# Delta rule: a 32-wide block inverse grown from the right, with the product W kept beside it

## The chip, the cores and the metric

One NeuronCore of one Trainium2 chip runs the whole program. The metric is the device time of one execution in microseconds, the median of the runs shown. Everything is float32; the large products are made from two rounded parts each (below).

## The reference, cut to what matters

One decoder layer: 256 tokens of width 2048 go through a wide input projection, two token mixers (gated DeltaNet and differential attention), their merge, an output projection with layer norm, and a SwiGLU feed-forward network with a second layer norm. The change is in the DeltaNet mixer, and there in one triangular solve:

```python
# per head and per chunk of C = 64 tokens; decay, beta, g as given
a_mat = jnp.where(strict, jnp.einsum('bhncd,bhnsd->bhncs', k_beta, k) * decay, 0.0)
rhs = jnp.concatenate([v * beta, k_beta * jnp.exp(g)[..., None]], axis=-1)
sol = lax.linalg.triangular_solve(a_mat + jnp.eye(C), rhs, left_side=True, lower=True, unit_diagonal=True)
u, w = sol[..., :dv], sol[..., dv:]
```

There are 16 heads and 4 chunks. The kernel does not solve; it forms the inverse T of (I + A) for each 64 x 64 block and multiplies by it.

## The kernel before, in words

**The stream of large products.** All weights pass through the core as 512 KB tiles of 256 x 512 numbers, in one fixed order, in a ring of four. For each tile ScalarE rounds the weights (`whi`, the function `split`, L800), VectorE takes the rest (`wlo`, L1204), and TensorE makes 12 matmuls of 512 columns (`gemm_tile`): high x high, high x low and low x high, for 2 blocks of rows by 2 blocks of tokens. `AHEAD = 3` tiles are split ahead of the one in use.

**Bodies and slots.** 32 tiles make a body, four groups of 8. A group accumulates into a pair of PSUM banks and is then copied out. After each tile of a body comes a *slot* 0 to 31: TensorE makes the tile's 12 matmuls, and then the small work that is written down for that slot. VectorE in each slot first makes its split, then (in this order) the scan step, the build step, the convolution and the turns of the slot; ScalarE likewise. Each engine works its list strictly in that order, and the engines are tied by counting semaphores only. The first four bodies (one for each four heads) carry the DeltaNet work. The first body is written out, the next three are one loop: scan of batch j-1 in slots 0 to 6, convolutions at slots 8 to 26 (`CONV_SLOTS`), build of batch j in slots 12 to 28. Four bodies with the differential attention follow, one for the last gate, then the branch, output and feed-forward projections.

**The inverse of before.** A batch has 8 matrices of 128 x 128 (4 heads by 2 token halves), each with two 64 x 64 blocks, each of those with two 32 x 32 blocks on its diagonal. `sub(q)` is the q-th 32-wide band. In slot 15 VectorE forms `AT` (the transposed A), takes the pairs on its diagonal blocks and forms the first `TTc` (transposed inverse) and `Tc` (its transpose). Rounds 0 to 3 double the inverted width from 2 to 32. A round has two TensorE places, one slot apart, slots 17 to 24: the even slot multiplies `AT` by `Tc` into a bank, VectorE masks that into `Pc`; the odd slot multiplies `Pc` by `TTc`, VectorE subtracts it from `TTc` and transposes into `Tc`. Each of these places has 32 products of 32 x 32 x 32, four independent ones (q = 0 to 3) side by side for each of the 8 matrices. The fifth round (slots 25 and 26) joins two 32-wide inverses to a 64-wide off-diagonal block, with 16 products a place. A float32 product is two MATMUL records in the trace.

**What is behind it.** In slot 25 ScalarE copies the diagonal blocks to `TTf` and `T` (`act_tt`). In slots 27 and 28 two places of 64 x 64 products join the 64-wide halves; the second one (`B<-TTf,Pm` and `B<-Pm`) waits for ScalarE's copies into `Pm` (`act_p21`), which stand on ScalarE's list behind the SiLU (L903) of the convolution of slots 24 and 26. VectorE also turns V blocks (L1421, `V_TURN`) and, in the loop, blocks of the output of the batch before (L1492, `OT_TURN`), at fixed slots.

`ch(...)` is a VectorE instruction followed by VectorE's own wait for its end.

Of the kernel before, what the change touches and what calls it, by code (L numbers as in the profile page):

```python
# [18 lines left out]
ALU = mybir.AluOpType  # L19
# [21 lines left out]
PV_SLOTS = [5, 11, 17, 23]  # L41
OH_SLOTS = [9, 15, 21, 27]
OT2_SLOTS = [11, 17, 23, 29]
CONV_LINKS, BUILD_LINKS, SCAN_LINKS, DA_LINKS = 12, 13, 7, 25
OT_SLOTS = (12, 14)
OT_TURN = {11: 3, 12: 4, 14: 2, 18: 1, 20: 3, 21: 3}
OT_HI = 29
V_TURN = {21: 1, 22: 3, 23: 3, 27: 3, 28: 2, 29: 2, 30: 1, 31: 1}
TURN = range(1, 7)
# [4 lines left out]
ROWS = range(2, 6)  # L54
WARM = 2
LATE_LO = 4
ROUNDS = 5
TPG = KC // TK
RING = 4
AHEAD = 3  # L60
# [39 lines left out]
def build(nc, xT, xrow, weights, w_ab, consts, early, params, lam_in, ln_in, out):  # L100
# [8 lines left out]
    with ctx:  # L109
# [14 lines left out]
        T = tmp("T", [P, 8, CH])  # L124
        Pm = tmp("Pm", [P, 8, CH])
        Tc = tmp("Tc", [P, 8, SB])
        TTc = tmp("TTc", [P, 8, SB])
        Pc = tmp("Pc", [P, 8, SB])
        masks = tmp("masks", [P, 7, SB])
        vr = tmp("vr", [P, 2, HB, P])  # L130
# [56 lines left out]
        B4 = [b[:, :].rearrange("p (h d) -> p h d", h=HB) for b in B]  # L187
        B8 = [b[:, :].rearrange("p (h d) -> p h d", h=8) for b in B]
        C8 = [b[:, 0:8 * SB].rearrange("p (h d) -> p h d", h=8) for b in B]

        def conv_bank(kind, half):

# [52 lines left out]
        def end_at(s):  # L245
# [23 lines left out]
            dve_lnT dve_x1 pe_x1T act_x1f act_x1T dve_x1T pe_y act_beta act_glo act_var dve_var act_root act_sig act_xn pro_chain ln_chain""".split()  # L269

        counted = """pe_conv dve_conv act_silu dve_cw act_tap
            dve_g rows pe_dt act_decay pe_ktok act_sqk dve_ktail pe_kk dve_at dve_t act_tt pe_p dve_p pe_t
            pe_p21 act_p21 pe_x21 act_x21 dve_vT dve_v pe_kq dve_qk
            pe_z dve_vn pe_so act_s act_o0 pe_ks dve_r pe_o1 dve_o1 pe_qtok act_osq act_sqq
            dve_oh dve_od pe_oT act_oT dve_oT
# [121 lines left out]
        def _(pe):  # L397
# [112 lines left out]
            def dn_build(j, s):  # L510
# [18 lines left out]
                if s == 14:  # L529
# [4 lines left out]
                            kc = cT[:, 0, h, t * P:(t + 1) * P]  # L534
                            last = mm(B4[2 + t][:, h, :], kc, kc)
                    last.then_inc(N["pe_kk"], 1)
                if 17 <= s < 17 + 2 * ROUNDS:
                    r, odd = divmod(s - 17, 2)
                    if not odd:
                        pe.wait_ge(N["dve_t"], 1 + (ROUNDS + 1) * j + r + 1)  # L540
                        waits_end()
                        for i in range(8):
                            if r < ROUNDS - 1:
                                for q in range(4):
                                    a = sub(q)
                                    last = mm(C8[1][a, i, :], AT[a, i, a], Tc[a, i, :])
                            else:
                                for q in (0, 2):
                                    last = mm(C8[1][sub(q + 1), i, :], AT[sub(q), i, sub(q + 1)], Tc[sub(q), i, :])
                        last.then_inc(N["pe_p"], 1)  # L550
                    else:
                        pe.wait_ge(N["dve_p"], 1 + ROUNDS * j + r + 1)
                        waits_end()
                        for i in range(8):
                            if r < ROUNDS - 1:
                                for q in range(4):
                                    a = sub(q)
                                    last = mm(C8[2][a, i, :], Pc[a, i, :], TTc[a, i, :])
                            else:
                                for q in (0, 2):  # L560
                                    b = sub(q + 1)
                                    last = mm(C8[2][sub(q), i, :], Pc[b, i, :], TTc[b, i, :])
                        last.then_inc(N["pe_t"], 1)
                if s == 27:
                    pe.wait_ge(N["dve_t"], 1 + (ROUNDS + 1) * (j + 1))
                    pe.wait_ge(N["act_tt"], 1 + j + 1)
                    waits_end()
                    for i in range(HB):
                        mm(B8[1][CH:P, i, :], AT[0:CH, i, CH:P], T[0:CH, i, :])
                        last = mm(B8[1][0:CH, HB + i, :], AT[0:CH, HB + i, CH:P], T[0:CH, HB + i, :])  # L570
                    last.then_inc(N["pe_p21"], 1)
# [226 lines left out]
        def _(act):  # L798
# [106 lines left out]
            def dn_build(j, s):  # L905
# [23 lines left out]
                                                        accum_out=d_("ss")[:, i:i + 1])  # L929
                        last.then_inc(N["act_sqk"], 1)  # L930
                if s == 25:
                    act.wait_ge(N["dve_t"], 1 + (ROUNDS + 1) * j + ROUNDS)
                    for q in range(4):
                        a = slice(q * SB, (q + 1) * SB)
                        copy(TTf[a, :, a], TTc[a])
                    for q in range(2):
                        a = slice(q * SB, (q + 1) * SB)
                        last = copy(T[a, :, a], Tc[a])
                    last.then_inc(N["act_tt"], 1)
                if s == 27:  # L940
                    act.wait_ge(N["dve_t"], 1 + (ROUNDS + 1) * (j + 1))
                    act.wait_ge(N["act_tt"], 1 + j + 1)
                    copy(Pm[0:CH, 0:HB, :], TTf[CH:P, HB:8, CH:P])
                    act.wait_ge(N["pe_p21"], 1 + j + 1)
                    copy(Pm[CH:P, 0:HB, :], B8[1][CH:P, 0:HB, :])
                    copy(Pm[0:CH, HB:8, :], B8[1][0:CH, HB:8, :]).then_inc(N["act_p21"], 1)
# [253 lines left out]
        def _(dve):  # L1200
# [56 lines left out]
            def prologue(s):  # L1257
# [7 lines left out]
                    tt(pz[0:4 * HEADS, 3, :], ident[0:4 * HEADS, 0:2 * HEADS], ident[0:4 * HEADS, 2 * HEADS:4 * HEADS],  # L1265
                       ALU.add).then_inc(N["dve_two"], 1)
                if s == 11:
                    m0, e0 = CONST["pairs"][0], CONST["eye"][0]
                    for q in range(4):
                        a, f = slice(q * SB, (q + 1) * SB), q % 2 * SB  # L1270
                        V.tensor_copy(masks[a, 0:6, :], cst[a, m0:m0 + 6 * CH].rearrange("p (m c) -> p m c", c=CH)
                                      [:, :, f:f + SB])
                        V.tensor_copy(masks[a, 6, :], cst[a, e0 + f:e0 + f + SB])
                if s == 4:
                    a0 = CONST["negdist"][0]
                    pro(ts(c("same"), cst[:, a0:a0 + P], -1e9, ALU.is_ge))
                    pro(tt(c("after"), c("same"), ident, ALU.subtract))
                    pro(ts(c("same"), c("after"), -1.0, ALU.mult, 1.0, ALU.add))
                    V.tensor_copy(after_r[:, :], c("after"))
                    lv = vda[:, 0, 0:4 * CH].rearrange("p (a b d) -> p a b d", a=2, b=2)  # L1280
                    pro(tt(vda[:, 1, 0:2 * CH].rearrange("p (a d) -> p a d", a=2), lv[:, :, 0, :], lv[:, :, 1, :], ALU.mult))
                    V.tensor_reduce(lam[:, :], vda[:, 1, 0:2 * CH].rearrange("p (a d) -> p a d", a=2), X, ALU.add
                                    ).then_inc(N["dve_lam"], 1)
# [81 lines left out]
            def dn_build(j, s, ch):  # L1365
# [11 lines left out]
                    seed(d_("rk"), d_("ss")).then_inc(N["dve_ss"], 1)  # L1377
                if s == 14:
                    dve.wait_ge(N["act_decay"], 1 + j + 1)
                    dve.wait_ge(N["pe_p21"], 1 + j)  # L1380
                    ch(tt(AT[:, :, :], decm[:, :, :], bc(d_("e"), P), ALU.mult))
                if s == 15:
                    dve.wait_ge(N["pe_kk"], 1 + j + 1)
                    for t in range(TOK):
                        last = tt(AT[:, 4 * t:4 * t + 4, :], B4[2 + t], AT[:, 4 * t:4 * t + 4, :], ALU.mult)
                    last.then_inc(N["dve_at"], 1)
                    dve.wait_ge(N["dve_at"], 1 + j + 1)
                    for q in range(4):
                        a = slice(q * SB, (q + 1) * SB)
                        last = tt(TTc[a], AT[a, :, a], rep(masks[:, 0, :], 8)[a], ALU.mult)  # L1390
                    ch(last)
                    ch(tt(TTc[:, :, :], rep(masks[:, 6, :], 8), TTc[:, :, :], ALU.subtract))
                    V.transpose(flat(Tc[:, :, :]), flat(TTc[:, :, :])).then_inc(N["dve_t"], 1)
                if 17 <= s < 17 + 2 * ROUNDS:
                    r, odd = divmod(s - 17, 2)
                    if not odd:
                        dve.wait_ge(N["pe_p"], 1 + ROUNDS * j + r + 1)
                        if r < ROUNDS - 1:
                            tt(Pc[:, :, :], C8[1], rep(masks[:, r + 2, :], 8), ALU.mult).then_inc(N["dve_p"], 1)
                        else:  # L1400
                            V.tensor_copy(Pc[:, :, :], C8[1]).then_inc(N["dve_p"], 1)
                    else:
                        dve.wait_ge(N["pe_t"], 1 + ROUNDS * j + r + 1)
                        if r < ROUNDS - 1:
                            ch(tt(TTc[:, :, :], TTc[:, :, :], C8[2], ALU.subtract))
                            V.transpose(flat(Tc[:, :, :]), flat(TTc[:, :, :])).then_inc(N["dve_t"], 1)
                        else:
                            for q in (0, 2):
                                a, b = (slice((q + o) * SB, (q + o + 1) * SB) for o in range(2))
                                ins = ts(TTf[a, :, b], C8[2][a], -1.0, ALU.mult)  # L1410
                            ch(ins)
                            V.transpose(T[SB:CH, :, 0:SB], TTf[0:SB, :, SB:CH]).then_inc(N["dve_t"], 1)
                if s == 25:
                    ch(tt(decm[:, :, :], decm[:, :, :], rep(c("same"), 8), ALU.mult))
                if s in V_TURN:
# [525 lines left out]
```

## Time and profile before

| | |
|---|---|
| median of 3 runs | 1940.16 us (1940.04 to 1940.58) |
| span of the profiled execution | 1937.5 us; the profile lists no device time of its own, so the distance from the runs' median is 2.7 us |
| granted TensorE clock, mean | 0.998 of full speed |
| TensorE busy | 1922.7 us, 99% |
| VectorE busy | 1365.1 us, 70% |
| ScalarE busy | 935.0 us, 48% |
| the four DeltaNet bodies | about the first 460 us |

In an answer of the trace "x64" is the number of records that were merged in the row, and the time in brackets is how long the engine was idle before it, with what ended that. The chain is the work that ended last, followed back from the end, each piece with its start, its length and its engine and line. All small products are recorded at the helper's line L399, so they are told apart by their tiles.

### The profile page before, as it was taken

How to read it: one execution, taken by the hardware profiler on the slowest of the kernel's cores; microseconds unless marked ns; L12 is line 12 of the kernel's file. 1: busy time of each engine (PE TensorE's matmuls, PEld its weight loads, DVE VectorE, ACT ScalarE, POOL GpSimd, SP SyncE). 2: the span in 40 equal slices, each digit the busy share in tenths (PEclk: the TensorE clock that was granted, in tenths of full speed). 3: DMA queues.
4: the chain of work that ended last, by engine and by line, in shares of the span. 5: the costliest groups of instructions: out<-in, count | busy, mean ns of one | idle time of the engine just before them, and what ended most of it. 6: DMA issues, size and time to landing. Idle time of an engine off the chain costs nothing.

```text
span 1937.5 us, 33061 instructions
## 1 busy us (share of the span) xinstructions
PE 1922.7 (99%) x11140; PEld 1581.1 (82%) x11140; DVE 1365.1 (70%) x1961; ACT 935.0 (48%) x1331; POOL 101.1 (5%) x296
## 2 busy tenths in 40 slices
PE   9999999999999999999999999999999999999997
PEld 7888887888888888888888888888888888888886
DVE  7779889797857777776566766577675466665556
ACT  6555565554455545455544445644443444443442
POOL 0102020010101111111000000000000000000000
PEclk9999999999999999999999999999999999999999
DMA  7444444444554545455655676555555555656555
GB/s 267 154 142 158 149 152 142 154 153 142 186 179 159 188 161 191 159 189 174 190 192 194 216 239 200 181 194 191 191 194 195 194 193 188 196 195 194 194 189 174
DMA packets 98013, 353.19 MB, mean 182 GB/s; under 512 B 10832, under 2 KB 11120, under 8 KB 97776
## 3 DMA queue, kind: packets, MB, share of 16 engines
q1 hardware_dynamic: 97904, 351.65, 55.4%
q8 instruction: 79, 1.29, 0.3%
q14 instruction: 30, 0.25, 0.0%
HBM read 349.51 MB, written 2.10 MB: 181 GB/s over the span
## 4 chain that ended last, share of the span: by engine, by line
PE 95%; DVE 2%; ACT 1%; issue 1%; DMA 1%; SPq 0%; DVEq 0%; ACTq 0%
PE pg L399 88%; PE B L399 5%; DVE gates L1212 1%; DMA raw<-in_weights 1%; PE B L493 0%; ACT whi L800 0%; DVE wlo L1204 0%; PE B L657 0%; ACT hraw L1086 0%; PE B L527 0%; ACT gates L1074 0%; PE B L666 0%; PE B L622 0%; ACT vda L1086 0%; ACT act_a L800 0%
## 5 line engine op out<-in xcount | busy, mean ns | idle before, releaser
L1204 DVE TENSOR_TENSOR wlo<-raw,whi 128x1024 fp32r<-128x1024 f32 (+1 forms) x640 | 779.4, 1221 | 452.1 <-ACT whi L800 433.8
L800 ACT ACTIVATE whi<-raw 128x1024 fp32r<-128x1024 f32 (+1 forms) x640 | 674.4, 1058 | 684.6 <-PE pg L399 673.0
L399 PE MATMUL pg<-whi,act_x 128*128 128x512 f32 x2960 | 950.5, 394 | 1.5 <-ACT whi L800 1.2
L399 PEld LDWEIGHTS pg<-whi,act_x 128*128 128x128 f32 x2960 | 555.3, 188 | 124.3 <-issue 8.9
L399 PE MATMUL pg<-wlo,act_x 128*128 128x512 f32 x1480 | 574.7, 390 | 0.0
L399 PE MATMUL pg<-whi,act_a 128*128 128x512 f32 x1632 | 504.8, 389 | 0.5 <-DVE act_a L1204 0.5
L399 PEld LDWEIGHTS pg<-whi,act_a 128*128 128x128 f32 x1632 | 306.3, 188 | 64.8 <-DVE act_a L1204 1.3
L399 PEld LDWEIGHTS pg<-wlo,act_x 128*128 128x128 f32 x1480 | 278.3, 188 | 53.3
L399 PE MATMUL pg<-wlo,act_a 128*128 128x512 f32 x816 | 317.5, 389 | 0.0
L399 PEld LDWEIGHTS pg<-wlo,act_a 128*128 128x128 f32 x816 | 153.2, 188 | 31.7
L399 PE MATMUL pg<-whi,act_b 128*128 128x512 f32 x512 | 158.4, 389 | 0.0
L399 PEld LDWEIGHTS pg<-whi,act_b 128*128 128x128 f32 x512 | 96.1, 188 | 20.0
L399 PE MATMUL pg<-wlo,act_b 128*128 128x512 f32 x256 | 99.6, 389 | 0.0
L1602 DVE STREAM_TRANSPOSE soft<-hraw 32x256 f32<-32x256 f32 x208 | 90.6, 435 | 3.8
L1212 DVE SCALAR_TENSOR_TENSOR cT<-B,cw,cT 128x255 f32<-128x255 f32 (+1 forms) x144 | 62.4, 475 | 2.9 <-ACT cT L898 1.0
L399 PEld LDWEIGHTS pg<-wlo,act_b 128*128 128x128 f32 x256 | 48.0, 188 | 9.9
L1011 ACT ACTIVATE soft<-soft,sm 128x128 f32<-128x128 f32 (+1 forms) x64 | 28.4, 446 | 38.2 <-DVE sm L1208 38.2
L876 ACT ACTIVATE hraw<-pg 128x512 f32<-128x512 f32 x40 | 21.8, 596 | 41.9 <-PE pg L399 36.6
L898 ACT ACTIVATE cT<-B,cw 128x256 f32<-128x256 f32 x48 | 20.1, 471 | 38.4 <-PE B L493 38.4
L1181 POOL TENSOR_SCALAR half<-half 128x2 f32<-128x2 f32 (+1 forms) x72 | 36.3, 505 | 6.3
L1179 POOL TENSOR_TENSOR half<-dsm 128x8 f32<-128x8 f32 x24 | 9.0, 373 | 446.4 <-DVE dsm L1209 445.1
L1179 POOL TENSOR_TENSOR half<-sm 128x2 f32<-128x2 f32 x48 | 12.0, 249 | 357.2 <-DVE sm L1209 354.7
(230 smaller groups left out, 1106.5 us busy)
## 6 DMA issues: line engine op xcount, KB each, us to landing
raw<-in_weights SPq DMA_DIRECT2D x646, 512.0 KB, 3.8
gates<-in_ln_in SPq DMA_DIRECT2D x4, 512.0 KB, 5.9
gates<-in_ln_in SPq DMA_DIRECT2D x1, 2048.0 KB, 8.4
out<-gates SPq DMA_DIRECT2D x8, 256.0 KB, 2.8
raw<-in_weights SPq DMA_DIRECT2D x4, 256.0 KB, 4.6
cT<-in_xT SPq DMA_DIRECT2D x2, 512.0 KB, 7.2
qT<-in_xrow SPq DMA_DIRECT2D x2, 512.0 KB, 7.4
kT<-in_xrow SPq DMA_DIRECT2D x2, 512.0 KB, 6.3
```

The costliest lines, as they stand in the source:

```text
L399: return nc.tensor.matmul(o, l, r, start=start, stop=stop)
L800: return nc.scalar.activation(o, i, ACT.Copy, scale=scale)
L876: last = nc.scalar.activation(dst(t), pg[pair][t][:, :], func, scale=scale)
L898: last = nc.scalar.activation(cT[:, kind, h, :], conv_bank(kind, half)[:, i * SEQ:(i + 1) * SEQ], ACT.Copy, scale=cw[:, kind, h, CONV - 1: ...
L1011: last = nc.scalar.activation(pr[:, m, a:b], pr[:, m, a:b], ACT.Exp, bias=sm[:, 28 + i:29 + i], accum_out=sm[:, 32 + i:33 + i])
L1179: ch(G.tensor_tensor(a, o, o, ALU.mult))
L1181: ch(G.tensor_scalar(a, a, -0.5, 1.5, ALU.mult, ALU.add))
L1204: return V.tensor_tensor(o, a, b, op)
L1212: return V.scalar_tensor_tensor(out=o, in0=a, scalar=s, in1=b, op0=op0, op1=op1)
L1602: ins = V.transpose(blocks_out(turned)[b * SB:(b + 1) * SB, :, :, a, :], blocks_in[a * SB:(a + 1) * SB, :, :, b, :])
```

## The change: what it does

It takes another route to the same 32 x 32 inverses. `TTc` goes. Two tiles of 32 columns lie side by side in `Pm`: `TT = Pm[:, :, 0:32]` is the transposed inverse, and `WT = Pm[:, :, 32:64]` a transposed product W that begins as the strictly triangular part of `AT`. Each level makes one TensorE place in place of two: the masked part `Pc` of W's transpose multiplies TT and WT together (64 columns; 32 columns in the first level, which needs only WT, and in the last, which needs only TT), and VectorE subtracts the result from both. There are five such places, in slots 17, 19, 20, 21 and 22 (`GROW`), and the off-diagonal places move from slots 25 and 26 to 23 and 24 (`OFF_P`, `OFF_T`). VectorE's work for a middle level is a subtraction over 128 x 512, a transpose and a mask product, in one chain, all in one slot. `OT_TURN` changes from {11: 3, 12: 4, 14: 2, 18: 1, 20: 3, 21: 3} to {11: 3, 12: 4, 14: 2, 17: 2, 19: 2, 20: 2, 21: 1}. The wait of slot 14 is for `pe_x21` now, since `Pm` is read until then.

```diff
-CONV_LINKS, BUILD_LINKS, SCAN_LINKS, DA_LINKS = 12, 13, 7, 25
+CONV_LINKS, BUILD_LINKS, SCAN_LINKS, DA_LINKS = 12, 19, 7, 25
-OT_TURN = {11: 3, 12: 4, 14: 2, 18: 1, 20: 3, 21: 3}
+OT_TURN = {11: 3, 12: 4, 14: 2, 17: 2, 19: 2, 20: 2, 21: 1}
-ROUNDS = 5
+GROW = {17: 0, 19: 1, 20: 2, 21: 3, 22: 4}
+GROWN = len(GROW)
+OFF_P, OFF_T = 23, 24
+        TT, WT = Pm[:, :, 0:SB], Pm[:, :, SB:CH]
 # TensorE
-                if 17 <= s < 17 + 2 * ROUNDS:
...
+                if s in GROW:
+                    k = GROW[s]
+                    f0, f1 = SB if k == 0 else 0, SB if k == GROWN - 1 else CH
+                    pe.wait_ge(N["dve_x"], 1 + GROWN * j + k + 1)
+                    waits_end()
+                    for i in range(8):
+                        for q in range(4):
+                            a = sub(q)
+                            last = mm(B8[1][a, i, f0:f1], Pc[a, i, :], Pm[a, i, f0:f1])
+                    last.then_inc(N["pe_x"], 1)
+                if s == OFF_P:
+                    pe.wait_ge(N["dve_t"], 1 + 2 * j + 1)
...
+                if s == OFF_T:
+                    pe.wait_ge(N["dve_p"], 1 + j + 1)
...
 # VectorE, slot 14
-                    dve.wait_ge(N["pe_p21"], 1 + j)
+                    dve.wait_ge(N["pe_x21"], 1 + j)
 # VectorE, slot 15
-                        last = tt(TTc[a], AT[a, :, a], rep(masks[:, 0, :], 8)[a], ALU.mult)
+                        last = tt(WT[a], AT[a, :, a], rep(masks[:, 1, :], 8)[a], ALU.mult)
                     ch(last)
-                    ch(tt(TTc[:, :, :], rep(masks[:, 6, :], 8), TTc[:, :, :], ALU.subtract))
-                    V.transpose(flat(Tc[:, :, :]), flat(TTc[:, :, :])).then_inc(N["dve_t"], 1)
+                    ch(tt(Tc[:, :, :], WT, rep(masks[:, 0, :], 8), ALU.mult))
+                    V.transpose(flat(Pc[:, :, :]), flat(Tc[:, :, :])).then_inc(N["dve_x"], 1)
+                    ch(tt(TT, rep(masks[:, 6, :], 8), Tc[:, :, :], ALU.subtract))
+                if s in GROW:
+                    k = GROW[s]
+                    dve.wait_ge(N["pe_x"], 1 + GROWN * j + k + 1)
+                    if k == GROWN - 1:
+                        ch(tt(TT, TT, B8[1][:, :, 0:SB], ALU.subtract))
+                        V.transpose(Tc[:, :, :], TT).then_inc(N["dve_t"], 1)
+                    else:
+                        if k == 0:
+                            ch(tt(WT, WT, B8[1][:, :, SB:CH], ALU.subtract))
                         else:
+                            ch(tt(Pm[:, :, :], Pm[:, :, :], B8[1], ALU.subtract))
+                        ch(V.transpose(Tc[:, :, :], WT))
+                        tt(Pc[:, :, :], Tc[:, :, :], rep(masks[:, k + 2, :], 8), ALU.mult).then_inc(N["dve_x"], 1)
+                if s == OFF_P:
+                    dve.wait_ge(N["pe_p"], 1 + j + 1)
+                    V.tensor_copy(Pc[:, :, :], C8[2]).then_inc(N["dve_p"], 1)
+                if s == OFF_T:
+                    dve.wait_ge(N["pe_t"], 1 + j + 1)
...
+                    V.transpose(T[SB:CH, :, 0:SB], TTf[0:SB, :, SB:CH]).then_inc(N["dve_t"], 1)
```

In the first body's slot 11 the mask of the pairs is joined by a mask of the whole strict triangle. ScalarE's waits of slots 25 and 27 follow the new counts, and its copies read `TT` in place of `TTc`.

## Rows read from the trace of the kernel before

**Rows 1.** The page, parts 1 and 4: busy time; the chain by engine.
```profile
PE 1922.7 (99%) x11140; PEld 1581.1 (82%) x11140; DVE 1365.1 (70%) x1961; ACT 935.0 (48%) x1331; POOL 101.1 (5%) x296
...
PE 95%; DVE 2%; ACT 1%; issue 1%; DMA 1%; SPq 0%; DVEq 0%; ACTq 0%
```
**Rows 2.** Waits of TensorE over the span: total, times, longest; the largest.
```profile
PE B L399 <- DVE TTf L1234: 1.5, 1, 1.5
```
**Rows 3.** The chain, first body (first two rows) and third: start, length, piece.
```profile
57.67 5.46 PE pg L399 x24
...
77.65 0.68 PE B L399 x50
...
304.50 0.68 PE B L399 x50
...
308.11 0.68 PE B L399 x50
...
326.55 0.44 PE B L493 x4
...
330.55 0.61 PE B L399 x16
...
334.11 0.05 issue
```
**Rows 4.** Groups by form, TensorE and VectorE: busy us, mean ns of one.
```profile
L399 PE MATMUL B<-Tc,AT 32*32 32x32 f32 x1152 | 14.8, 194 | 0.0
...
L399 PE MATMUL B<-T,AT 64*64 64x64 f32 x64 | 2.7, 224 | 0.0
...
L1204 DVE TENSOR_TENSOR AT<-B,AT 128x512 f32<-128x512 f32 x8 | 5.1, 682 | 0.0
```
**Rows 5.** Timeline of TensorE, second body: a place of slot 25; that of slot 27.
```profile
209.30 0.69 PE L399 MATMUL B<-Tc,AT 32*32 32x32 f32 x32
...
216.88 0.68 PE L399 MATMUL B<-T,AT 64*64 64x64 f32 x16
```
**Rows 6.** Timeline of VectorE, third body, slots 17 to 19.
```profile
296.36 0.42 DVE L1204 TENSOR_TENSOR Pc<-B,masks 128x256 f32<-128x256 f32 x1
296.69 1.22 DVE L1204 TENSOR_TENSOR wlo<-raw,whi 128x1024 fp32r<-128x1024 f32 x1
297.95 0.42 DVE L1204 TENSOR_TENSOR TTc<-TTc,B 128x256 f32<-128x256 f32 x1
298.41 0.45 DVE L1406 STREAM_TRANSPOSE Tc<-TTc 128x256 f32<-128x256 f32 x1
298.78 2.64 DVE L1212 SCALAR_TENSOR_TENSOR cT<-B,cw,cT 128x255 f32<-128x255 f32 x6
301.45 0.43 DVE L1492 STREAM_TRANSPOSE qT<-od 32x256 f32<-32x256 f32 x1
301.90 1.23 DVE L1204 TENSOR_TENSOR wlo<-raw,whi 128x1024 fp32r<-128x1024 f32 x1
303.04 0.42 DVE L1204 TENSOR_TENSOR Pc<-B,masks 128x256 f32<-128x256 f32 x1
```
**Rows 7.** The same view of the first body, slot 19.
```profile
75.63 0.42 DVE L1204 TENSOR_TENSOR Pc<-B,masks 128x256 f32<-128x256 f32 x1
```
**Rows 8.** Timelines of VectorE and ScalarE, third body, slots 25 to 28.
```profile
324.95 1.22 DVE L1204 TENSOR_TENSOR decm<-decm,cst 128x1024 f32<-128x1024 f32 x1
...
327.66 0.85 DVE L1208 TENSOR_SCALAR TTf<-B 32x256 f32<-32x256 f32 x2
...
329.01 2.69 DVE L1212 SCALAR_TENSOR_TENSOR cT<-B,cw,cT 128x255 f32<-128x255 f32 x6
...
331.73 1.06 ACT L903 ACTIVATE cT<-cT 128x1024 f32<-128x1024 f32 x1 [2.91 <-DVE cT L1212]
...
333.25 0.77 ACT L800 ACTIVATE Pm<-B 64x256 f32<-64x256 f32 x2
```

More of the change, by code:

```diff
@@ L126, in build @@
         Tc = tmp("Tc", [P, 8, SB])
-        TTc = tmp("TTc", [P, 8, SB])
         Pc = tmp("Pc", [P, 8, SB])
@@ L271, in build @@
         counted = """pe_conv dve_conv act_silu dve_cw act_tap
-            dve_g rows pe_dt act_decay pe_ktok act_sqk dve_ktail pe_kk dve_at dve_t act_tt pe_p dve_p pe_t
+            dve_g rows pe_dt act_decay pe_ktok act_sqk dve_ktail pe_kk dve_at dve_t act_tt dve_x pe_x pe_p dve_p pe_t
             pe_p21 act_p21 pe_x21 act_x21 dve_vT dve_v pe_kq dve_qk
@@ L536, in dn_build @@
                     last.then_inc(N["pe_kk"], 1)
-                if 17 <= s < 17 + 2 * ROUNDS:
[L538 to L563, printed above, removed]
@@ new lines, in dn_build @@
+                if s == OFF_P:
+                    pe.wait_ge(N["dve_t"], 1 + 2 * j + 1)
+                    waits_end()
+                    for i in range(8):
+                        for q in (0, 2):
+                            last = mm(C8[2][sub(q + 1), i, :], AT[sub(q), i, sub(q + 1)], Tc[sub(q), i, :])
+                    last.then_inc(N["pe_p"], 1)
+                if s == OFF_T:
+                    pe.wait_ge(N["dve_p"], 1 + j + 1)
+                    waits_end()
+                    for i in range(8):
+                        for q in (0, 2):
+                            b = sub(q + 1)
+                            last = mm(C8[1][sub(q), i, :], Pc[b, i, :], TT[b, i, :])
+                    last.then_inc(N["pe_t"], 1)
@@ L564, in dn_build @@
                 if s == 27:
-                    pe.wait_ge(N["dve_t"], 1 + (ROUNDS + 1) * (j + 1))
+                    pe.wait_ge(N["dve_t"], 1 + 2 * (j + 1))
                     pe.wait_ge(N["act_tt"], 1 + j + 1)
@@ L931, in dn_build @@
                 if s == 25:
-                    act.wait_ge(N["dve_t"], 1 + (ROUNDS + 1) * j + ROUNDS)
+                    act.wait_ge(N["dve_t"], 1 + 2 * j + 1)
                     for q in range(4):
                         a = slice(q * SB, (q + 1) * SB)
-                        copy(TTf[a, :, a], TTc[a])
+                        copy(TTf[a, :, a], TT[a])
                     for q in range(2):
@@ L940, in dn_build @@
                 if s == 27:
-                    act.wait_ge(N["dve_t"], 1 + (ROUNDS + 1) * (j + 1))
+                    act.wait_ge(N["dve_t"], 1 + 2 * (j + 1))
                     act.wait_ge(N["act_tt"], 1 + j + 1)
@@ L1267, in prologue @@
                 if s == 11:
-                    m0, e0 = CONST["pairs"][0], CONST["eye"][0]
+                    m0, e0, i0 = (CONST[n][0] for n in ("pairs", "eye", "incl"))
+                    levels = cst[:, m0:m0 + 6 * CH].rearrange("p (m c) -> p m c", c=CH)
                     for q in range(4):
                         a, f = slice(q * SB, (q + 1) * SB), q % 2 * SB
-                        V.tensor_copy(masks[a, 0:6, :], cst[a, m0:m0 + 6 * CH].rearrange("p (m c) -> p m c", c=CH)
-                                      [:, :, f:f + SB])
+                        V.tensor_copy(masks[a, 0, :], levels[a, 0, f:f + SB])
+                        V.tensor_copy(masks[a, 2:6, :], levels[a, 2:6, f:f + SB])
                         V.tensor_copy(masks[a, 6, :], cst[a, e0 + f:e0 + f + SB])
+                        tt(masks[a, 1, :], cst[a, i0 + f:i0 + f + SB], cst[a, e0 + f:e0 + f + SB], ALU.subtract)
                 if s == 4:
@@ L1389, in dn_build @@
                         a = slice(q * SB, (q + 1) * SB)
-                        last = tt(TTc[a], AT[a, :, a], rep(masks[:, 0, :], 8)[a], ALU.mult)
+                        last = tt(WT[a], AT[a, :, a], rep(masks[:, 1, :], 8)[a], ALU.mult)
                     ch(last)
-                    ch(tt(TTc[:, :, :], rep(masks[:, 6, :], 8), TTc[:, :, :], ALU.subtract))
-                    V.transpose(flat(Tc[:, :, :]), flat(TTc[:, :, :])).then_inc(N["dve_t"], 1)
[L1394 to L1399, printed above, removed]
-                        else:
[L1401 to L1412, printed above, removed]
@@ new lines, in dn_build @@
+                if s == OFF_P:
[3 more added lines that the diff above has]
+                    dve.wait_ge(N["pe_t"], 1 + j + 1)
+                    for q in (0, 2):
+                        a, b = (slice((q + o) * SB, (q + o + 1) * SB) for o in range(2))
+                        ins = ts(TTf[a, :, b], C8[1][a], -1.0, ALU.mult)
+                    ch(ins)
+                    V.transpose(T[SB:CH, :, 0:SB], TTf[0:SB, :, SB:CH]).then_inc(N["dve_t"], 1)
```

## The prediction

> **What bounds the kernel now.** I read the page first: TensorE is busy 99% of the span and carries 95% of the chain that ended last; VectorE has 70%, which says nothing yet of single stretches [rows 1]. Then the waits of TensorE: over the whole span the largest is 1.5 us, at the very start, before any weight is there [rows 2]. So the time is the sum of what TensorE is given to do, in the order in which it is given, and a change is worth what it takes off that list, less each wait that it puts in. The chain of waits shows the list piece by piece: two tiles with nothing between take 5.46 us, so a tile is 2.73; from one place of small products to the next is 304.50 to 308.11, 3.61 us [rows 3]. Last I read VectorE's timeline at the slots in question, for the stretch decides and not the 70%.
>
> **Term 1, TensorE's own work.** A full place of before (32 products, 64 records) costs 3.61 - 2.73 = 0.88 us. The half place of slot 26 stands behind transposes of 0.44: 326.55 to 330.55 is 4.00, less 0.44 and 2.73 is 0.83. The 64 x 64 place of slot 27 costs 334.11 - 330.55 - 2.73 = 0.83 [rows 3].
> A place of 32 products with 64 columns does not occur before. The half place is 16 products, two side by side for 8 matrices, so 16 passes one after the other, and takes 0.69 us; the 64 x 64 place has 8 passes in a row and takes 0.68 [rows 5]. With the length of a single last pass off (0.19 and 0.22, [rows 4]), a pass of 32 columns takes (0.69 - 0.19) / 16 = 0.031 us and one of 64 columns (0.68 - 0.22) / 8 = 0.058. The four bands of a full place run beside each other (0.88 with twice the products of 0.83), so a wide place is the half place and 16 x 0.027 + 0.03 more: 0.83 + 0.46 = 1.29. Bounds: 0.88, the narrow full place, where width cost nothing; 2.2, if the bands ran two at a time, twice 16 x 0.058 + 0.22 with 0.14 around it. I take 1.29, since it is the cadence of a pass of the same width.
> Per body before: 8 x 0.88 + 2 x 0.83 = 8.70. After: levels 0 and 4 are narrow, 2 x 0.88; levels 1 to 3 wide, 3 x 1.29; two half places, 1.66: 7.29. That is 1.41 a body, 5.6 us over four bodies, if no wait appears.
> The Trainium skill ("TensorEngine Tiling (Array Packing)", "Instruction Overhead") says that a matmul has some 60 cycles of overhead and that one with a free dimension of 1 has the latency of one with 60; by it 64 columns would cost next to what 32 do. The rows do not bear that out for a row of passes: 0.031 against 0.058 [rows 4, 5]. What it would make of the time is the second rival below.
>
> **Term 2, a wait in slot 20.** In the loop's three bodies VectorE has no idle time between slots 16 and 19; the second half of that stretch stands in [rows 6], where each row starts as the last ends. What the change adds there moves everything behind it. I use the distance from one start to the next: chained 128 x 256 product 0.46 (297.95 to 298.41), transpose 0.37 (to 298.78), unchained mask product 0.33 (296.36 to 296.69), one turn 0.45 (301.45 to 301.90), split 1.14 (301.90 to 303.04) [rows 6]. Slot 15: one subtraction more behind the signal, +0.46. Slot 17: before one mask product, 0.33; after a subtraction 0.46, a chained transpose 0.48, a mask product 0.33 and two turns 0.90, so +1.84. Slot 18: before 0.46 + 0.37 and a turn 0.45, after none of them, -1.28; the splits and convolutions meet different neighbours, which takes off 0.2 more (the convolution's 2.67 falls to 2.59, and the split before it from 1.26 to 1.14). So VectorE reaches level 1 in slot 19 at 303.04 + 0.8 = 303.85. There stands 128 x 512 (0.69 [rows 4], 0.72 with its chain), transpose 0.48, product 0.42: Pc is ready at 305.5, and 0.1 later TensorE can start (334.02, where ScalarE's last copy ends [rows 8], to the chain's next piece at 334.16 is 0.14 [rows 3]).
> TensorE wants level 2 one slot later, in slot 20. The place there was at 304.50 [rows 3]; slot 18 lost a place (-0.88) and slot 19 has a wide one (+0.41): 304.0. The wait is 305.6 - 304.0 = 1.6 us. Of the stated bounds, 0 is an engine that catches up by slot 19, and 2.2 is the sum with durations in full in place of distances. I take 1.6, since the stretch has no slack that could be used up first. In the first body there are no turns of the batch before, and the same sum gives another result: VectorE's level 1 starts at 75.63 [rows 7] + 0.46 + 0.94 - 0.83 - 0.9 of waits that go with the removed place + small ones, some 75.2, its product is there at 76.8, and TensorE wants it at 77.65 - 0.5 = 77.15 [rows 3, 7]: no wait. So 3 x 1.6 = 4.8 us.
> Behind it VectorE has work of 1.14 + 1.64 + 0.90 = 3.7 us in slots 20 and 21, against 2.73 + 1.29 = 4.0 for TensorE: the lag closes, and levels 3 and 4 wait for nothing (0.4 and 0.9 us to spare).
>
> **Term 3, slot 28.** The second 64 x 64 place waits for `act_p21` already (0.05 [rows 3]). Its chain is VectorE's convolution of slot 26 to its end at 331.70, SiLU from 331.73, copies to 334.02 [rows 8]: 2.46 from the convolution's end to 334.16. After the change the last off-diagonal place is in slot 24, in front of the convolution of that slot on VectorE's list, which before had none in front. From the transposes of such a slot the join is at +1.11 (326.55 to 327.66), the convolution at +2.46 (329.01) [rows 3, 8], then 2.6, split 1.14, the `decm` product 1.25 to 1.4, split 1.14, convolution 2.69: +11.35, and +2.46 is +13.8. TensorE arrives at 4.00 + 2.73 + 3.19 + 3.56 = +13.5. A wait of 0.33, 0.28 more than now, in all four bodies: 1.1 us. Bounds 0 and 2.4 (0.6 a body, durations in full).
>
> **Nothing**: ScalarE's copies (same number and shape, in slot 25, whose input is there a slot or more earlier); the wait of slot 14 for `pe_x21` (made half a body before); the masks in slot 11 of the first body (some 1 us of VectorE; slot 12 has idle time, and if that were gone it would be up to 1 us once); the order of splits (three tiles ahead, 8 us of cover; if it were gone, each late split stops TensorE by its lateness). VectorE's own sum rises by about 2 us a body, and only where it is behind does that show.
>
> **Sum**, against the profiled execution's span of 1937.5, whose distance to the median of the runs, 2.7 us, is taken as fixed: -5.6 + 4.8 + 1.1 = +0.3, span 1937.8, time 1940.4 us.
>
> **Rivals.**
> 1. The wait in slot 20 does not come (VectorE is early enough there, by idle time that goes elsewhere or turns that overlap): -5.6 + 1.1 = -4.5, 1935.7. For it: a lag of 0.8 us in 12 us of list is little, and waits in between can absorb it. Against it: no idle time in that stretch in the loop's bodies.
> 2. Wide places at the price of narrow ones (0.88): -3 x 0.41 x 4 = -4.9 more, but in the loop's bodies level 1's gain makes the wait in slot 20 longer by the same 0.41 (+1.2): 1940.4 - 3.7 = 1936.7. Against it the cadence of the 64-column passes.
> 3. Slower: the wide places run two bands at a time, 2.2 us each. Its place is levels 1 to 3. The slot-20 wait takes in one of the three in the loop's bodies (1.6 - 0.91 is still above 0), so 9 x 0.91 = 8.2 us: 1948.6. It decides from a place of about 1.75 us on (9 x 0.46 = 4 us). Against it: four bands of 32 columns do overlap now, 0.88 for twice the products of 0.83.
>
> **Chances.** Forecast 0.66, rival 1 0.18, rival 2 0.08, rival 3 0.08. A measurement of this kernel tells about 0.2% (3.9 us) from no change, so 1936.3 and 1944.0 are the limits. Faster: most of rival 1 and part of rival 2, 0.22; slower: rival 3 and little of the forecast, 0.09; within: 0.69. The range of 8 in 10 reaches down to rival 1 and up to terms 2 and 3 at their upper bounds (3 x 0.6 and 1.3 more): 1935.5 to 1943.5.
>
> **What would show it.** In the loop's bodies TensorE idle before the place of slot 20, 1.6 us, ended by VectorE's product into Pc; none in the first body. Wide places (64 records of 32 x 64) at 1.29 us of TensorE's list. Idle time before `B<-TTf,Pm` of 0.3 us a body. The chain of waits then shows VectorE lines in slots 18 and 19 of three bodies, which it does not have now. The forecast is wrong if TensorE's waits in the four bodies sum to under 3 us, or if a wide place costs under 1.1 or over 1.5.

## The result, and the profile after

The changed kernel takes 1944.77 us, median of 9 runs (1941.73 to 1946.11), against 1939.81 us, median of 9 runs of the kernel before beside it (1939.42 to 1940.58). The ratio is 1.0024, with a 95% interval of 1.0016 to 1.0032: it is slower. The forecast was 1940.4 us in a range of 1935.5 to 1943.5, that is next to no change (+0.3 us on the span); the measured loss is 5 us, outside the range. The first thing to see is the spread: the runs of before lie within 1.2 us, those of the changed kernel within 4.4.

The profiled execution took 1945.53 us with a span of 1943.8, 6.3 us more than the span before. These are the waits of TensorE in it (total, times, longest), to be held against [rows 2]:

```profile
PE B L401 <- DVE Pc L1204: 5.8, 3, 1.9
PE B L401 <- ACT Pm L800: 1.5, 4, 0.4
PE B L401 <- DVE TTf L1234: 1.5, 1, 1.5
```

One wait is new and one has grown, both at the places that the prediction named: three times 1.93 us for VectorE's `Pc` in slot 20, and four times up to 0.4 us for ScalarE's copies into `Pm` in slot 28, 1.5 us in all where the kernel before had 0.2. TensorE's groups by form show the other side, fewer records and a new shape (busy us, mean ns of one; idle before), against [rows 4]:

```profile
L401 PE MATMUL B<-Pm,Pc 32*32 32x64 f32 x768 | 14.6, 228 | 5.8 <-DVE Pc L1204 5.8
...
L401 PE MATMUL B<-Pm,Pc 32*32 32x32 f32 x640 | 8.8, 193 | 0.0
...
L401 PE MATMUL B<-Tc,AT 32*32 32x32 f32 x128 | 2.8, 192 | 0.0
```

VectorE's timeline of the third body, slots 17 to 19, answers [rows 6]:

```profile
298.20 0.42 DVE L1204 TENSOR_TENSOR Pm<-Pm,B 128x256 f32<-128x256 f32 x1
298.65 0.45 DVE L1408 STREAM_TRANSPOSE Tc<-Pm 128x256 f32<-128x256 f32 x1
299.13 0.42 DVE L1204 TENSOR_TENSOR Pc<-Tc,masks 128x256 f32<-128x256 f32 x1
299.58 0.88 DVE L1499 STREAM_TRANSPOSE qT<-od 32x256 f32<-32x256 f32 x2
300.48 1.23 DVE L1204 TENSOR_TENSOR wlo<-raw,whi 128x1024 fp32r<-128x1024 f32 x1
301.62 2.68 DVE L1212 SCALAR_TENSOR_TENSOR cT<-B,cw,cT 128x255 f32<-128x255 f32 x6
304.22 1.22 DVE L1204 TENSOR_TENSOR wlo<-raw,whi 128x1024 fp32r<-128x1024 f32 x1
305.35 0.68 DVE L1204 TENSOR_TENSOR Pm<-Pm,B 128x512 f32<-128x512 f32 x1
306.07 0.45 DVE L1408 STREAM_TRANSPOSE Tc<-Pm 128x256 f32<-128x256 f32 x1
306.55 0.43 DVE L1204 TENSOR_TENSOR Pc<-Tc,masks 128x256 f32<-128x256 f32 x1
```

There is no idle time in brackets anywhere: VectorE works without a break from slot 17 on, and `Pc` is ready at 306.98. TensorE's timeline of the same stretch shows what that does, and something more:

```profile
304.56 0.39 PE L401 MATMUL pg<-wlo,act_x 128*128 128x512 f32 x1
304.79 0.39 PE L401 MATMUL pg<-whi,act_x 128*128 128x512 f32 x1
307.12 1.67 PE L401 MATMUL B<-Pm,Pc 32*32 32x64 f32 x64 [1.94 <-DVE Pc L1204]
308.72 0.79 PE L401 MATMUL pg<-whi,act_x 128*128 128x512 f32 x1
309.31 0.63 PE L401 MATMUL pg<-wlo,act_x 128*128 128x512 f32 x1
309.74 1.05 PE L401 MATMUL pg<-whi,act_x 128*128 128x512 f32 x2
...
311.42 0.39 PE L401 MATMUL pg<-wlo,act_x 128*128 128x512 f32 x1
311.65 0.62 PE L401 MATMUL pg<-whi,act_x 128*128 128x512 f32 x2
```

The wait is 1.94 us. Behind it a matmul of 512 columns has 0.43 us to the next start (309.31 to 309.74), near twice the 0.23 in front of the wait (304.56 to 304.79), and 2 us later it is 0.23 again (311.42 to 311.65). Busy time by stretch (PE, PEld, DVE, ACT, POOL), then the granted clock, the DMA share and GB/s, says why:

```profile
301.00:307.00 6.00, 4.18 (x77) 3.11 (x76) 5.83 (x11) 3.23 (x4) 0.00 (x0) 1.00 0.35 109
307.10:310.50 3.40, 3.38 (x68) 2.94 (x69) 3.30 (x6) 0.19 (x1) 0.00 (x0) 0.55 0.37 139
```

Through the wait the granted clock is 1.00; then it is 0.55 over 3.4 us, that is nearly all of it at the lower of the two levels, 1.2 GHz in place of 2.4. In half-microsecond stretches the clock stands at 0.50 from 307.5 to 310.5 us and at 1.00 again from 311.0. Work that takes 1.7 us at the upper level takes 3.4. In this execution it happened behind all three waits of slot 20 (the stretches from 191.0, 307.1 and 422.9 us), and behind none of the waits of slot 28. The mean clock of the span fell from 0.998 to 0.995. The 0.998 of the kernel before is not a loss in its work: the granted clock is below 1.00 only in its last 8 us, where TensorE has nothing more to do (0.53 from 1929 to 1937 us). The nine runs follow it roughly: the two at 0.995 took 1945.5 and 1945.9 us, the six at 0.996 between 1943.1 and 1946.1, the one at 0.997 took 1941.7. So the profiled execution is one of the longer ones of the nine, 0.8 us over their median.

The account of the 6.3 us of the span: TensorE's own work. A wide place costs 1.235 us by the distance of starts and a narrow one 0.886. The first body shows the difference, 3.98 us from a wide place to the next start and 3.64 from a narrow one, each with one tile of weights in it:

```profile
81.14 1.09 PE L401 MATMUL B<-Pm,Pc 32*32 32x64 f32 x64
...
85.12 0.75 PE L401 MATMUL B<-Pm,Pc 32*32 32x32 f32 x64
...
88.76 0.69 PE L401 MATMUL B<-Tc,AT 32*32 32x32 f32 x32
```

So a body's inverse takes 2 x 0.886 + 3 x 1.235 + 2 x 0.836 = 7.15 where it took 8 x 0.886 + 2 x 0.836 = 8.76: -1.6, in four bodies -6.4. Waits in slot 20 +5.8, in slot 28 +1.3, the clock 3 x 1.7 = +5.1. The sum is +5.8; the remaining 0.5 us is not traced.

### The profile page after: what moved, and what is told of

Its sections match the earlier page's. It is cut to its first block, busy times and chain, and to the rows that moved or that the text cites. A ratio compares the mean times of both kernels' runs of the same rounds, so it can differ in the third digit from the quotient of the medians.

```text
span 1943.8 us, 31547 instructions
## 1 busy us (share of the span) xinstructions
PE 1922.1 (99%) x10372; PEld 1581.6 (81%) x10372; DVE 1374.5 (71%) x1981; ACT 934.4 (48%) x1331; POOL 101.1 (5%) x296
## 4 chain that ended last, share of the span: by engine, by line
PE 90%; DVE 5%; issue 2%; ACT 2%; DMA 0%; SPq 0%; DVEq 0%; ACTq 0%
PE pg L401 84%; PE B L401 5%; DVE cT L1212 1%; DVE wlo L1204 1%; DVE gates L1212 1%; ACT whi L800 0%; DVE Pm L1204 0%; DVE AT L1204 0%; DMA raw<-in_weights 0%; ACT QKT L928 0%; PE B L495 0%; PE B L657 0%; ACT Pm L800 0%; DVE decm L1204 0%; ACT hraw L1086 0%
## 5 line engine op out<-in xcount | busy, mean ns | idle before, releaser
L401 PEld LDWEIGHTS B<-Pm,Pc 32*32 32x32 f32 x1408 | 19.9, 109 | 13.7 <-issue 13.7
```

What stands on the lines that cost most here:

```text
L401: return nc.tensor.matmul(o, l, r, start=start, stop=stop)
```

## The experiments

Experiments 1, 3 and 4 are held against 23 runs of the kernel before (median 1939.43 us), experiments 2, 5, 6 and 7 against 27 (1939.77 us). The diffs leave out the constants that only count semaphore signals.

**1. The wait alone, in the kernel before.** Nothing of the change; VectorE gets extra work in slot 19 that changes no value. The diff is of the long one; the short one has `range(3)`.

```diff
+                if s == 19:
+                    for i in range(4):
+                        if isinstance(j, int):
+                            ch(V.tensor_copy(sm[:, 64:65], lam[:, 0:1]))
+                        else:
+                            hf = slice(4 * (i % 2), 4 * (i % 2) + 4)
+                            ch(tt(decm[:, hf, :], decm[:, hf, :], rep(c("same"), 4), ALU.mult))
```

The long one (four products):

> The kernel of before with nothing of the change: only VectorE gets four more chained 128x512 products (0.72 us each; they repeat a mask product on decm, so no value changes) in slot 19 of the loop's three bodies, ahead of the product that TensorE waits for in slot 20. 2.9 us of work less about 0.85 us of slack: TensorE waits about 2.0 us, three times. Theory (clock): after a wait of that length the granted TensorE clock falls to half for about 3.4 us, as in the changed kernel, which costs 1.5 to 1.7 us more each time: 6.1 + 4.8, about 1950.5 us. Rival (the wait alone): a wait costs its length, and what the changed kernel lost beyond that has another cause in it: 1945.9 us, clock at full speed throughout.

Measured: 1948.42 us, median of 4 runs (1946.86 to 1950.09), ratio 1.0048 (1.0031 to 1.0065), 9.0 us over before. The waits in its profile, and the stretches with the wait or behind it in the second, the third and the fourth body (there the wait ends at 427.19 us):

```profile
PE B L399 <- DVE Pc L1204: 6.4, 3, 2.1
```
```profile
192.60:198.00 5.40, 5.18 (x76) 3.94 (x76) 4.51 (x8) 0.00 (x0) 0.00 (x0) 0.68 0.31 100
...
306.50:312.00 5.50, 3.40 (x74) 2.53 (x73) 5.21 (x9) 1.23 (x2) 0.00 (x0) 0.85 0.30 101
421.00:430.00 9.00, 6.86 (x151) 5.28 (x151) 8.60 (x16) 3.06 (x3) 0.00 (x0) 1.00 0.30 111
```

The clock falls behind the first two waits and not behind the third (1.00 there up to 440 us), though all three are 2.1 us long. Nor does it fall at the same distance: TensorE works again from 192.82 and from 309.80 us, and the clock is at the lower level from 194.3 to 197.7 and from 310.4 to 313.8. So a plain wait brings the clock down, without anything of the change, but not every time. The kernel lands between the two expectations (1950.5 and 1945.9), with a spread of 3.2 us in four runs; neither holds as it was put.

The short one (three products):

> The same with three products, 2.15 us: TensorE waits about 1.3 us, three times. If the clock stays up, both theories give 1943.8 us. If it falls here too, 1948.5. The step from this one to the one with four products is 2.2 us if only waits count, and up to 6.8 if the clock falls in the longer one alone.

Measured: 1944.27 us, median of 8 runs (1943.04 to 1945.48), ratio 1.0026 (1.0016 to 1.0037). Its waits, and the stretch behind the first:

```profile
PE B L399 <- DVE Pc L1204: 4.2, 3, 1.4
```
```profile
192.00:197.40 5.40, 4.90 (x142) 3.96 (x143) 5.19 (x10) 1.19 (x2) 0.00 (x0) 1.00 0.36 138
```

Three waits of 1.4 us, 4.2 together, cost 4.8 us, close to their length, with the clock at 1.00 behind each of them. The step to the long one is 4.15 us for 2.2 us more of waits.

**2. The same wait, with TensorE busy in it.** The changed kernel, with nothing moved.

```diff
+                if s == 20 and not isinstance(j, int):
+                    for i in range(8):
+                        mm(B[3][:, :], act_x[:, 0, 0, 0:P], flat(act_x[:, 0, 0:2, :]))
```

> The changed kernel, and nothing moved or removed: TensorE only gets eight matmuls of 512 columns more (8 x 0.227 = 1.81 us, into a bank that nobody reads then, with operands at rest) in slot 20 of the loop's three bodies, ahead of its wait. They fit into the 1.93 us in which it is idle now. Theory (clock): the wait's end does not move, TensorE is not idle before it, the clock stays up, and the 1.5 us behind each wait are saved: about 1944.8 - 4.6 = 1940.2 us, and the runs lie within 1 us or so of each other. Rival (the wait has its price by itself, whatever TensorE does in it; or the changed kernel's loss lies elsewhere): 1944.8 us or a little more, for 24 more matmuls.

Measured: 1941.17 us, median of 10 runs (1940.30 to 1942.55), ratio 1.0009 (0.9999 to 1.0018): 3.6 us less than the changed kernel in its own runs, by adding work, and 1.0 us over the theory's 1940.2. TensorE's timeline in the second body, and the stretch behind it:

```profile
189.15 1.98 PE L401 MATMUL B<-act_x 128*128 128x512 f32 x8
191.22 1.10 PE L401 MATMUL B<-Pm,Pc 32*32 32x64 f32 x64
192.25 0.50 PE L401 MATMUL pg<-whi,act_x 128*128 128x512 f32 x1
```
```profile
191.00:196.40 5.40, 5.30 (x142) 4.25 (x142) 5.21 (x10) 1.46 (x2) 0.00 (x0) 1.00 0.52 181
```

The place of slot 20 starts as it did 0.15 us behind the end of VectorE's `Pc` (191.07 to 191.22, in the changed kernel 190.84 to 190.99), so the wait's end has not moved. Its records take 1.10 us, where the three of the changed kernel took 1.60, 1.67 and 1.42, and the clock is 1.00 over the whole 460 us of the four bodies. The ten runs lie within 2.3 us, where within 1 was expected. This is the direct test: the lateness of VectorE is untouched, only TensorE's idleness is gone, and with it 3.6 of the 4.3 us that the median of the changed kernel lies above its own work and waits (+5.0 us, less the -6.4 + 5.8 + 1.3 of the account above).

**3. A shorter wait in the changed kernel.**

```diff
-OT_TURN = {11: 3, 12: 4, 14: 2, 17: 2, 19: 2, 20: 2, 21: 1}
+OT_TURN = {11: 3, 12: 4, 14: 2, 19: 2, 20: 2, 21: 1, 28: 2}
```

> The changed kernel with VectorE's two output turns of slot 17 (0.9 us) moved to slot 28: TensorE's wait in slot 20 of the loop's bodies falls from 1.93 to about 1.0 us. Rival (the wait alone): 0.9 x 3 = 2.7 us less than the changed kernel, about 1942 us. Theory (clock): if the clock no longer falls, another 4.7 us less, about 1937.5 us, and the runs agree within 0.5 us where those of the changed kernel spread over 4 us.

Measured: 1939.67 us, median of 10 runs (1938.80 to 1940.25), ratio 1.0001 (0.9992 to 1.0011), all at a mean clock of 0.998 or 0.999. That is 5.1 us less for 0.9 us of VectorE's work moved in three bodies, near twice the 2.7 that this takes off the waits by its length. It is 2.2 us short of the expectation, and the spread is 1.45 us, not 0.5. The waits name the rest:

```profile
PE B L401 <- DVE Pc L1204: 2.7, 3, 0.9
PE pg L401 <- DVE wlo L1204: 2.3, 3, 1.1
PE B L401 <- ACT Pm L800: 1.5, 4, 0.4
```

The second row is new: the two turns in slot 28 make ScalarE's copy of `qT` in slot 29 wait (7.4 us in three waits, none of them there in the changed kernel or in experiment 6), and the splits behind it are late for TensorE. So TensorE's waits fell by only 0.8 us in all (3.1 less, 2.3 more), and the time by 5.1.

**4. No wait in slot 20.** Level 2 gets a slot more.

```diff
-GROW = {17: 0, 19: 1, 20: 2, 21: 3, 22: 4}
+GROW = {17: 0, 19: 1, 21: 2, 22: 3, 23: 4}
-OFF_P, OFF_T = 23, 24
+OFF_P, OFF_T = 24, 25
-OT_TURN = {11: 3, 12: 4, 14: 2, 17: 2, 19: 2, 20: 2, 21: 1}
+OT_TURN = {11: 3, 12: 4, 14: 2, 17: 2, 20: 2, 21: 1, 28: 2}
```

> The changed kernel with levels 2 to 4 one slot later (slots 21 to 23), the off-diagonal places in 24 and 25, and the output turns at 17: 2, 20: 2, 21: 1, 28: 2. VectorE then has a slot more for level 1 and TensorE should not wait there at all. TensorE's own work is that of the changed kernel. Theory (clock): 1944.8 - 5.8 (waits) - 4.7 (clock) = 1934.3 us, if slot 28 does not wait longer than it does in the changed kernel (0.4 us a body). Rival (the wait alone): 1939.0 us.

Measured: 1936.82 us, median of 10 runs (1936.29 to 1938.05), ratio 0.9987 (0.9978 to 0.9997). It lies 2.2 us under the rival's 1939.0, and 2.5 over the theory's 1934.3, which is what its own waits explain: 2.2 us for the splits, and 0.3 more than the changed kernel had in slot 28:

```profile
PE pg L401 <- DVE wlo L1204: 2.2, 2, 1.3
PE B L401 <- ACT Pm L800: 1.8, 3, 0.6
```

**5. The wait of slot 28.** To 4, one product moved behind the last convolution.

```diff
-                if s == 25:
+                if s == 27:
                     ch(tt(decm[:, :, :], decm[:, :, :], rep(c("same"), 8), ALU.mult))
```

> The kernel with level 2 in slot 21 (a_slot21, 1936.8 us), with VectorE's mask product on decm (1.25 us) moved from slot 25 to slot 27, behind the convolution of slot 26. The convolution then starts when its ScalarE input is there, 0.86 us earlier. Theory (slot 28 waits for the convolution of slot 26 by way of SiLU and the copies into Pm): the 0.66 us of idle time before the place of slot 28 goes in each body, up to 1.8 us as the waits add up: 1935.0. Rival (something behind slot 28 is late too and takes it back): unchanged, 1936.8, with the idle time later.

Measured: 1934.77 us, median of 10 runs (1933.73 to 1935.35), ratio 0.9974 (0.9965 to 0.9984): 2.05 us less. The row `PE B <- ACT Pm` is gone from its waits, and `PE pg <- DVE wlo` stands as it was, 2.2 us. The path that term 3 of the prediction followed is borne out: taking VectorE's product out of it took the wait away.

**6. The last waits.** To 5, other slots for three turns.

```diff
-OT_TURN = {11: 3, 12: 4, 14: 2, 17: 2, 20: 2, 21: 1, 28: 2}
+OT_TURN = {11: 3, 12: 5, 14: 2, 17: 2, 20: 1, 21: 1, 24: 2}
```

> As before, and the two turns of slot 28 (whose lateness makes ScalarE's copy of qT late in slot 29, and through it the splits: TensorE waits 1.1 us in two bodies) go to slots 12 and 24, one turn of slot 20 to 24. If these are the last waits, TensorE has its work of the changed kernel and no wait in the four bodies: 1939.4 - 6.4 = 1933.0 us. If the new slots make VectorE late in slots 17 to 27, TensorE waits there and the time is 1935 or more.

Measured: 1933.74 us, median of 6 runs (1932.50 to 1934.07), ratio 0.9969 (0.9957 to 0.9982). It beats both kernels. The waits of TensorE in its whole span are near those of the kernel before, 3.9 us against 3.6; the largest rows:

```profile
PE B L401 <- DVE TTf L1234: 1.5, 1, 1.5
PE pg L401 <- ACT whi L800: 1.3, 3, 0.7
```

6.0 us less than the kernel before is what the change is worth with no new wait of its own, where the places counted up to 6.4 and the waits are 0.3 us longer.

**7. What width costs.** To 4, the last level 64 columns wide; the half that is added is read by nobody.

```diff
-                    f0, f1 = SB if k == 0 else 0, SB if k == GROWN - 1 else CH
+                    f0, f1 = SB if k == 0 else 0, CH
```

> a_slot21 with the last level (slot 23) 64 columns wide in place of 32; the half that it adds is read by nobody. If a pass of 64 columns costs what the wide places of the changed kernel show (1.24 us against 0.89), 0.34 more a body, 1.4 us in all: 1938.2. If the width of a place cost nothing by itself and the wide ones are longer for another reason (the 128x512 product that reads the same bank, say), unchanged, 1936.8, and 0.89 us a place.

Measured: 1937.21 us, median of 10 runs (1936.81 to 1938.33), ratio 0.9989 (0.9980 to 0.9999), 0.4 us over experiment 4, between the expectations and within its spread. By the time alone it is open; by the trace it is not: the last level starts at 199.60 us and the next piece of the list at 203.49, 3.89 us later, where experiment 4 has 199.96 to 203.48, 3.52. A 64-column place costs some 0.35 us more than a 32-column one (0.37 here), though half of its result is read by nobody. The groups by form of this kernel (first row) have 1024 records of the wide shape:

```profile
L401 PE MATMUL B<-Pm,Pc 32*32 32x64 f32 x1024 | 17.5, 216 | 0.1
```
```profile
PE B L401 <- ACT Pm L800: 0.7, 3, 0.2
```

The second fence says where 1.1 of the 1.4 us went: the wait of slot 28 was 1.8 us in experiment 4 and is 0.7 here. TensorE came later to a place where it had to wait anyway.

## Why the prediction was wrong, point by point

**The step that failed** is in term 2, where the wait in slot 20 was priced at its length: "So 3 x 1.6 = 4.8 us". It rests on the first paragraph's premise that a change is worth what it takes off TensorE's list, "less each wait that it puts in". The wait was there, in the three bodies and at the place named, with the engine and the tile named, and absent in the first body. Its price was not its length. In a stream where TensorE is next to never idle, 1.9 us without work was followed by about 3.4 us at the lower level of the granted clock, some 1.7 us lost each time in the profiled execution. Experiment 1 shows that a wait does this without the change, experiment 2 that the same lateness without idleness does not, and experiment 3 that 1 us less of wait gives back more than its length. The prediction had no rival in which the clock moves, and none of its signs of being wrong was set on it: the waits sum to over 3 us and a wide place costs between 1.1 and 1.5 as it said, so none of them points at what went wrong.

With three times 1.7 the forecast would be 1945.5, the time of the profiled run, but this agreement is in part luck. Other terms were off too and cancel: the places gave 0.8 us more than forecast (6.4 for 5.6), the waits cost 1.0 and 0.2 more, 0.5 us is not traced, and the distance from span to time, taken as 2.7, is 1.7 in the changed kernel (1943.8 and 1945.53). The runs of the kernel before that list both have 1.7 to 1.9 as well, so the profiled execution of 1937.5 was itself some 0.8 us quicker than their median.

The Trainium skill ("TensorE: Matmul & The Clock Gate", "HAM oscillation — how this bites in real kernels") tells of waits of some 3 to 5 us for a DMA between bursts of matmuls, behind which the next burst starts at the lower clock. The traces here show the like behind shorter waits for another engine, 1.9 to 2.1 us. Read as it stands, the section would not have warned of waits this short, but it names the rival that the prediction lacked on the slower side.

**The size of that wait**: 1.93 us against 1.6. Two rows of VectorE's list were longer than I took: slot 15's extra subtraction held it 0.58 us (292.75 to 293.33) against 0.46, and slot 17's mask product, which waits for the transpose in front of it, 0.45 (299.13 to 299.58) against the 0.33 of one that waits for nothing. The wide place in front of the wait cost 0.055 less than I took, so TensorE came earlier. Together that is 0.3 us a body, +1.0 us over three.

**Term 1**: right in kind, 0.055 us too high for a wide place (1.235 against 1.29), -0.66 us over twelve places. It gave 5.6 us; the places add up to 6.4, and experiment 6 brings 6.0. Rival 2 (width costs nothing) is out, by 1.235 against 0.886 and by experiment 7; rival 3 (two bands at a time, 2.2 us) is out by the same figure. The rule of the Trainium skill that the prediction cited ("TensorEngine Tiling (Array Packing)", "Instruction Overhead") does not give the price of such a place: single records of 32 and of 64 columns are near each other (193 and 216 ns), yet the place costs 0.886 and 1.235 us.

**Term 3**: right, 1.3 us against 1.1, by the path named, as experiment 5 shows.

**Rival 1** (VectorE early enough): out; VectorE's only idle time from slot 15 to slot 20 of the third body is 0.19 us, for the end of its own subtraction in slot 15.

**The range** held only cases in which TensorE's clock stays, so its upper end, 1943.5, lay inside what the changed kernel does (1941.7 to 1946.1).

## What to carry to other kernels

Where one engine is busy 99% of the time, each new wait of it has to be asked about twice: how long, and whether the engine's clock survives it. Here 1.4 us cost 1.6 us (experiment 1, medians) and 1.9 us cost 3.6 (the profile of the changed kernel). Before a chain on a second engine is lengthened, lay its list end to end against the first engine's schedule at each slot; a slot of delay from level 2 on, three turns and a mask product in other places turned 0.24% slower into 0.31% faster, with the arithmetic unchanged. And a wait further down the list takes back small gains and hides small losses ahead of it, as in experiment 7: read the price of a part from the distance of starts, not from the total.

## What the runs showed of the hardware that was not expected

- Behind a TensorE wait of 1.9 to 2.1 us, in a stream with next to no other gaps, the granted clock was at its lower level for about 3.4 us: in 3 of 3 cases of the changed kernel's profile, in 2 of 3 of the long experiment. It fell 0.3 to 0.6 us after TensorE had begun to work again in four of the five and 1.5 us after in the fifth. Behind waits of 0.9 to 1.4 us it stayed up in all six cases seen (experiments 1 and 3). Nothing in the profile tells the third case of the long one from its first two, so which waits are hit stays open.
- A kernel with such waits has a wider spread of times, 4.4 us in 9 runs and 3.2 us in 4, against 1.2 us (9 runs) and about 2 us (23 and 27 runs) for the kernel before. The spread is a sign to look for the clock, but a weak one: the short experiment, with the clock up in its profile, spreads over 2.4 us in 8 runs.
- Eight matmuls of no use, 24 in all, made a kernel 3.6 us faster.
